# Moving one SBUF buffer by 64 bytes under a 512-byte boundary in a fused transformer kernel

## The reference

```
for l in range(2):
    x = x + 0.5 * rms(swiglu(rms(x), w_in, w_out))          # 1024 -> 2 x 2816 -> 1024
    x = x + rms(token_mixer(rms(x), mem, ...))               # conv, sparse attention, memory attention
    x = x + 0.5 * rms(swiglu(rms(x), w_in, w_out))
x = ssd_dilated_layer(x, ...)                                # rms(x) @ w_in, scan, attention, @ w_out
x = moba_layer(x, ...)                                       # rms(x) @ w_in, attention, @ w_out
```

## Time and profile before

| | |
|---|---|
| median of three executions | 1794.52 us (1793.49 to 1795.93) |
| profiled execution | 1794.16 us |
| its span | 1792.4 us |
| TensorE matmuls busy | 1750.1 us, 98% of the span, 10552 instructions |
| TensorE weight loads busy | 1515.9 us, 85% |
| VectorE busy | 1245.0 us, 69% |
| ScalarE busy | 954.0 us, 53% |
| mean HBM read | 173 GB/s |

### The profile page before, as it was taken

One profiled execution on the slowest core, in us unless ns is written; L12 is line 12 of the kernel. 1 busy time (PEld: TensorE's weight loads), 2 busy tenths in 40 slices (PEclk: granted clock), 3 DMA queues, 4 the chain that ended last, 5 costly groups with the idle time before them and its releaser, 6 DMA issues. The chain is left out here.

```text
span 1792.4 us, 28470 instructions
## 1 busy us (share of the span) xinstructions
PE 1750.1 (98%) x10552; PEld 1515.9 (85%) x10552; DVE 1245.0 (69%) x2344; ACT 954.0 (53%) x1621; POOL 18.7 (1%) x20
## 2 busy tenths in 40 slices
PE   7999999999999999999999999999999999999998
PEld 6888789998888888888799988788879988758887
DVE  6666577567876667666666668766677885786775
ACT  5444454566554546445545665654556456463574
POOL 1000000000000000000000000000000000000000
PEclk9999999999999999999999999999999899999999
DMA  8455454534545454545546425455544444203531
GB/s 312 179 191 195 176 188 179 224 138 177 185 187 192 181 206 176 188 181 205 188 177 247 154 107 212 176 200 187 184 168 176 160 166 168 81 26 141 187 131 59
DMA packets 29905, 311.65 MB, mean 174 GB/s; under 512 B 3312, under 2 KB 3696, under 8 KB 4848
## 3 DMA queue, kind: packets, MB, share of 16 engines
q1 hardware_dynamic: 28944, 307.18, 46.2%
q0 software_dynamic: 864, 3.15, 0.6%
HBM read 309.26 MB, written 1.05 MB: 173 GB/s over the span
## 5 line engine op out<-in xcount | busy, mean ns | idle before, releaser
L490 ACT ACTIVATE region_r<-ring 128x1024 fp32r<-128x1024 f32 x495 | 515.3, 1055 | 365.6 <-PE psum L873 343.6
L496 DVE TENSOR_TENSOR ring_r<-ring,region_r 128x1024 fp32r<-128x1024 f32 x487 | 581.8, 1221 | 137.2 <-ACT region_r L490 130.8
L873 PE MATMUL psum<-xs_r,region_r 128*128 128x256 f32 (+1 forms) x3152 | 582.0, 333 | 2.2 <-ACT region_r L490 1.4
L873 PEld LDWEIGHTS psum<-xs_r,region_r 128*128 128x128 f32 x3152 | 475.7, 191 | 60.3 <-issue 9.7
L873 PE MATMUL psum<-xs_r,ring_r 128*128 128x256 f32 x2336 | 327.3, 283 | 0.0
L873 PEld LDWEIGHTS psum<-xs_r,ring_r 128*128 128x128 f32 x2336 | 312.2, 192 | 13.1
L873 PE MATMUL psum<-region_r 128*128 128x512 f32 (+1 forms) x944 | 300.9, 385 | 0.0
L873 PE MATMUL psum<-region_r,xs_r 128*128 128x512 f32 (+3 forms) x1088 | 280.5, 351 | 5.5 <-DVE region L2658 3.0
L873 PEld LDWEIGHTS psum<-region_r,xs_r 128*128 128x128 f32 x1088 | 192.0, 193 | 36.2 <-ACT xs_r L1779 4.5
L873 PEld LDWEIGHTS psum<-region_r 128*128 128x128 f32 (+1 forms) x944 | 174.0, 185 | 33.2
L873 PE MATMUL psum<-ring_r,region_r 128*128 128x512 f32 (+1 forms) x440 | 157.3, 375 | 0.0
(11 more groups left out here) (245 smaller groups left out, 1616.2 us busy)
## 6 DMA issues: line engine op xcount, KB each, us to landing
ring<-in_weights SPq DMA_DIRECT2D x192, 1536.0 KB, 6.4
gpost<-in_posts POOLq DMA_DIRECT2D x6, 512.0 KB, 4.8
cst<-in_const SPq DMA_DIRECT2D x1, 1213.0 KB, 22.7
xs<-in_mem SPq DMA_DIRECT2D x1, 1024.0 KB, 5.5
x<-in_x SPq DMA_DIRECT2D x1, 1024.0 KB, 7.9
out<-x SPq DMA_DIRECT2D x2, 512.0 KB, 2.6
pars<-in_par SPq DMA_DIRECT2D x1, 368.0 KB, 6.0
p<-in_par SPq DMA_DIRECT2D x1, 206.0 KB, 22.7
```

The costliest lines, as they stand in the source:

```text
L490: eng.activation(unit.high, unit.raw, ACT.Copy).then_inc(h_ready, 1)
L496: eng.tensor_tensor(unit.low, unit.raw, unit.high.bitcast(F32), ALU.subtract).then_inc(l_ready, 1)
L873: ins = pe.matmul(bank, lhsT, rhs, start=start, stop=stop)
```

## The change

One constant and two unused buffers are added. `before_xs` has 112 elements (448 bytes), `after_xs` 16 elements (64 bytes). `xs` then begins at byte 74688, 448 bytes above a multiple of 512, or 64 below the next one. Everything behind it moves up by 512 bytes (`gpost` to 91136, `region` to 121856, `cst` to 212480), so each of those stays on its multiple of 512. No instruction is added, removed or moved in the program.

```
-LINE, LEAD = 128, 96
+LINE, LEAD, SHIFT = 128, 96, 16
...
         x = sb("x", [P, NT, D])
+        sb("before_xs", [P, LINE - SHIFT])
         low_high, low_high_r = two_names("xs", [P, 2 * NT, D])
+        sb("after_xs", [P, SHIFT])
         gpost, gpost_r = two_names("gpost", [P, 2, D])
```

## The result

The changed kernel has a median of 1778.9 us (1775.35 to 1783.21, six runs) against 1794.01 us (1789.28 to 1795.93, six runs) of the kernel before: a ratio of 0.9922, with a 95% interval of 0.9903 to 0.994. That is 14 us or 0.8% less by the ratio, with an interval from 11 to 17 us (the two medians lie 15.1 us apart). The span of the profiled execution went from 1792.4 to 1779.9 us.

What follows compares the result with a forecast made beforehand. The prediction took TensorE's matmul pace, busy 98% of the span, as the bound. It took 6.3 us from pace and 2.7 us from the transient, 9 us together, off 1794.2 us: 1785 us, range 1758 to 1809.

Steps and rivals of the forecast that it cites:

- those two zeros: Transfer of `mem` into `xs` (0 to 2.4 us) and element-wise instructions on the buffer (under 1.7 us), each taken as 0.
- The forecast of 9 us: Small gain on matmuls reading `xs_r`: 6.3 us from pace plus 2.7 us from the transient; chance 0.38.
- the surplus: TensorE's time per matmul beyond its streamed columns: 31 to 32 cycles with aligned operands, 30 at scattered places.
- My list of what would show each case: Paces expected near 70 us in the feed-forward stretch, wide and narrow, for forecast, no effect, large gain and slower.
- large gain: Rival: stream and load never meet again; 20 to 43 us less, paces under 222 and near 116 ns; chance 0.12.
- slower: Rival: stream runs into the load each matmul; 1803 to 1820 us, paces over 227 or over 121 ns; chance 0.24.
- The bound on the gain: Most the matmuls reading `xs_r` could save: 23.9 us on 512 columns, 18.8 us on 256, together 43 us.
- The transient of the earlier trace: Eight wide feed-forward matmuls after narrow ones at 230 against 226 ns; about two per tile, 5 us, half counted.
- The step from a surplus that comes once per matmul to the weight load as its cause: Equal surplus at 512 and 256 columns, 31 and 32 cycles, was assigned to the weight load of each matmul.

Runs made afterwards that it cites:

- all64: Kernel before with the leading buffer 64 bytes shorter, so every buffer begins 64 bytes under a multiple of 512, distances unchanged: 1789.6 us (before: 1792.48).
- shift_320: Changed kernel with `xs` 320 instead of 64 bytes under a multiple of 512: 1781.4 us.
- ring_over_64: Kernel before with `xs` on its multiple of 512 and the ring (low weights) 64 bytes over one: 1797.5 us (before: 1789.2).
- shift_48: Changed kernel with padding meant for 48 bytes; as built, `xs` lies 32 under against the ring, 64 under against `region`: 1791.6 us (before: 1792.2).
- half_load: Kernel before, seven of eight feed-forward matmuls of each kind loading 64 of 128 stationary columns, half of those products left out: 1788.2 us (before: 1792.2).

## Why the prediction was right, and where it wasn't

The sign, the range (1758 to 1809) and the bottleneck were right: it was the pace of TensorE that changed. The transfer into `xs` landed in 5.6 us where it had 5.5, and the conversions on the buffer kept a median of 632 ns, so those two zeros held. The forecast of 9 us came out as 14 us. That these are near each other is luck: 14 us is what is left of a gain and a loss that the sum doesn't have.

The mechanism was right only in its first half. That a distance between streamed and stationary operand matters is shown (`all64`, `shift_320`, the narrow group of `ring_over_64`, and the groups of `shift_48`). Wrong was the step that gave one small saving of 0.9 ns to all 6976 matmuls, by taking the surplus out of its step. Measured was 4.4 ns saved on 4128 narrow ones (18.1 us) and 4.4 ns lost on 1360 wide ones (6.0 us), and nearly nothing where `xs_r` is stationary, the form from which the 0.9 ns had been taken. Near 70 us the paces are 234 and 115 ns, for a forecast of 224 to 225 and 118 to 119. My list of what would show each case named two paces for each case, and the outcome took the narrow pace of "large gain" and the wide pace of "slower" together. A mean over scattered places could not tell this: it mixes distances, and each form has its own answer to each.

The bound on the gain was wrong as well. I let the narrow form gain at most 4 ns, since 12 matmuls of 64 columns took 116 ns each. In the better rhythm it runs at 113.1 ns over sixteen, nearly 7 ns under before. Those twelve were measured from entry to exit and across the next form's start: one by one their starts lie 60 ns apart at the entry, 110 to 112 within and 205 at the exit, so the mean wasn't a floor.

The transient of the earlier trace rows was read rightly as a memory of what ran before, and then priced at 5 us, of which half went into the sum. It stands once for each feed-forward tile, not twice (84 groups of eight at 230 ns, each behind narrow ones, against 81 behind down products at 226 to 227), so it was worth 2.5 us. The memory itself was what the sum lacked: what ran before picks the rhythm. The step from a surplus that comes once per matmul to the weight load as its cause was too simple (`half_load`).

The Trainium skill, "TensorE: Matmul & The Clock Gate", section "Step-by-step: what each phase is for", has it that loading the next weights takes no read bandwidth from the running matmul, by which the place would be worth nothing. These runs don't bear that out for the one-pass format: moving one operand by 64 bytes, with no instruction changed, moved the paces of both forms, and 14 us. Whether it's bandwidth that the two reads take from each other no run shows.

## What to carry to other kernels

In a stream of one-pass float32 matmuls on TensorE, the distance between the streamed and the stationary operand in SBUF, modulo 256 bytes as far as tried here, is worth some nanoseconds for each matmul, with different signs for different widths. It costs a padding buffer to try, and no rule replaces trying: of the six distances tried only two, 64 and 320 bytes under, gained more than single executions spread. Look up in the built program where the buffers lie: here sizes were rounded up to 32 bytes, and one padding of 48 bytes moved everything behind it. Read the pace of each form from the timeline, not the total, and expect an edit of the order, or a wait, to switch a run of equal matmuls between two paces.

## What was not expected of the hardware

- At one distance (64 bytes) a run of equal 256-column matmuls has two steady paces, 113.1 and 117.5 ns, and splitting the matmul at its entry in two switches between them, in both directions.
- The second half of a 512-column stream lay at another distance (64 bytes under) without any effect on its steady pace (227.5 ns).
- Two 256-column matmuls with their own loads took 236 ns and one of 512 columns 234 ns at the same distance: splitting a wide stream was nearly free there (at distance 0 it would be 240 for 226).
- At 32, 96 and 128 bytes under, the single starts of the narrow ones near 71 us lie 115 to 122 ns apart without settling, where at 0 and at 64 they settle at 120 and at 113 to 114.
- Down products with both operands in `region` went from 293.3 to 296.8 us when only the ring, which the matmuls between them stream, moved by 64 bytes.
